# Before the experts of a two-block model: tokens transposed before their norm, a feature-major router, and a gather in full precision

## The reference, cut to what matters

```python
h = h + rms_norm(mix, post_mix_norm)
t = rms_norm(h, pre_ffn_norm)                      # x * rsqrt(mean(x*x) + eps) * gain, 256 x 1024
g_prob = softmax(t @ w_group_router + b_group)     # 4 groups
g_w, g_idx = top_k(g_prob, 1)
e_logits = (t @ w_expert_router + b_expert)        # 32 experts in 4 groups
e_w, e_idx = top_k(softmax(e_logits[group g_idx]), 2)
weights = g_w * e_w / sum(e_w)
hid = silu(t @ w_gate[e]) * (t @ w_up[e]) * weights      # experts, 1024 -> 256
routed = hid @ w_down[e]                                 # 256 -> 1024
shared = (silu(t @ w_sh_gate) * (t @ w_sh_up)) @ w_sh_down
h = h + rms_norm(routed + shared, post_ffn_norm)
```

## Time and profile before

| | |
|---|---|
| median of three runs | 1015.51 us (1015.17 to 1015.65) |
| profiled execution | 1013.33 us, its span 1011.7 us |
| busy over the span | PE 84%, DVE 52%, ACT 38%, POOL 4% |
| mean granted clock of TensorE | 0.901 of full |
| moved by DMA | 205.80 MB, mean 203 GB/s |

### The profile page before, as it was taken

How to read it: one execution, slowest core, us unless ns; L and a number is a source line. 1 busy time by engine, 2 the same in 40 slices (tenths; PEclk the granted TensorE clock), 3 DMA queues, 4 the chain that set the end, 5 groups by cost and what they waited for, 6 DMA issues and landing times.

```text
span 1011.7 us, 13380 instructions
## 1 busy us (share of the span) xinstructions
PE 848.5 (84%) x5447; PEld 665.3 (66%) x5447; DVE 525.3 (52%) x858; ACT 383.3 (38%) x635; POOL 40.2 (4%) x101
## 2 busy tenths in 40 slices
PE   5877799777867676658699999779999999999976
PEld 3877555676534343323699987548787899989964
DVE  2669841554210010201666579894577666666655
ACT  4434533433200001001645475453544543444334
POOL 3000000000111110010000000000000000000000
PEclk9889855958998987888799999798999999999988
DMA  9941102510999999999951845205555556655201
GB/s 273 386 136 42 42 1 99 187 68 1 386 417 417 415 417 417 418 418 386 286 180 43 304 155 208 94 1 197 198 163 170 167 173 204 203 170 174 77 1 42
DMA packets 82099, 205.80 MB, mean 203 GB/s; under 512 B 7836, under 2 KB 50980, under 8 KB 73844
## 3 DMA queue, kind: packets, MB, share of 16 engines
q1 hardware_dynamic: 69632, 151.46, 42.2%
q0 software_dynamic: 10064, 53.27, 13.1%
q10 hardware_dynamic: 2340, 0.18, 0.2%
HBM read 203.85 MB, written 1.05 MB: 203 GB/s over the span
## 4 chain that ended last, share of the span: by engine, by line
PE 61%; DMA 16%; DVE 15%; ACT 4%; issue 3%; POOL 0%; SPq 0%; ACTq 0%; DVEq 0%
DMA big<-in_w_gate 14%; PE ps L1797 8%; PE ps L1798 8%; PE ps L1799 8%; PE ps L1623 7%; PE ps L1625 7%; PE ps L1624 7%; PE ps L1882 4%; DMA big<-in_w_in 2%; DVE WL L1001 2%; PE ps L1741 1%; PE ps L1753 1%; DVE XT L1443 1%; DVE big L1483 1%; DVE WL L993 1%
## 5 line engine op out<-in xcount | busy, mean ns | idle before, releaser
L1001 DVE TENSOR_TENSOR WL<-big,WH 128x1024 fp32r<-128x1024 f32 x154 | 186.8, 1223 | 112.0 <-ACT WH L589 110.3
L1623 PE MATMUL ps<-XH,WH 128*128 128x256 f32 (+1 forms) x672 | 195.7, 291 | 5.4 <-DVE XL L1016 4.9
L589 ACT ACTIVATE WH<-big 128x1024 fp32r<-128x1024 f32 x154 | 160.8, 1054 | 89.5 <-PE ps L1799 88.6
L1624 PE MATMUL ps<-XL,WH 128*128 128x256 f32 (+1 forms) x672 | 193.2, 287 | 0.0
L1625 PE MATMUL ps<-XH,WL 128*128 128x256 f32 (+1 forms) x672 | 192.9, 287 | 0.0
L1623 PEld LDWEIGHTS ps<-XH,WH 128*128 128x128 f32 x672 | 130.7, 195 | 8.4 <-issue 6.1
L1624 PEld LDWEIGHTS ps<-XL,WH 128*128 128x128 f32 x672 | 130.9, 195 | 0.8
L1625 PEld LDWEIGHTS ps<-XH,WL 128*128 128x128 f32 x672 | 130.7, 195 | 0.0
L1797 PE MATMUL ps<-WH,XH 128*128 128x512 f32 x256 | 104.5, 408 | 12.0 <-DVE WL L993 5.0
L1882 PE MATMUL ps<-big 128*32 128x256 f32 x1024 | 75.3, 459 | 45.0 <-DMA big<-in_w_gate 31.1
L1798 PE MATMUL ps<-WH,XL 128*128 128x512 f32 x256 | 102.4, 400 | 0.0
(11 more groups left out here) (346 smaller groups left out, 1104.8 us busy)
## 6 DMA issues: line engine op xcount, KB each, us to landing
big<-in_w_in SPq DMA_DIRECT2D x35, 1024.0 KB, 9.2
big<-in_w_gate SPq DMA_DIRECT2D x16, 1024.0 KB, 14.8
big<-in_w_up SPq DMA_DIRECT2D x16, 1024.0 KB, 18.2
big<-in_w_gate POOLq DMA_DIRECT2D x16, 1024.0 KB, 19.3
big<-in_w_up POOLq DMA_DIRECT2D x16, 1024.0 KB, 22.7
big<-in_w_down SPq DMA_DIRECT2D x16, 1024.0 KB, 16.5
big<-in_w_down POOLq DMA_DIRECT2D x16, 1024.0 KB, 18.7
big<-in_w_mlp_up SPq DMA_DIRECT2D x16, 1024.0 KB, 5.5
```

Source lines behind the costliest of these rows:

```text
L589: s.activation(dst, src, ACT.Copy).then_inc(ev("unit_high"), 1)
L1001: v.tensor_tensor(dst, src, h.bitcast(F32), ALU.subtract).then_inc(ev("unit_split"), 1)
L1623: mm(o, h, rh, start=first, stop=False, skip_group_check=skip)
L1624: mm(o, h, rl, start=False, stop=False, skip_group_check=skip)
```

## The change

It has six parts.

1. `h_tok` plus the scaled projection is written into `h1`; the transposes read `h1` unnormed as soon as `h_mixed` counts. XH and XL hold the unnormed features times the gain. The reciprocal root `st(5)` is made once and multiplied in afterwards: into the logits, into the silu and the product of the shared expert, into the gathered rows.
2. The router is feature-major: `router_hi` and `router_lo` are the stationary side (36 columns), the 256 tokens move; 24 matmuls of 256 columns instead of 48 of 36 and the bias rows. The 36x256 result is copied to SBUF, transposed back by two small matmuls, and scaled with the bias added (`b_router` is now broadcast to 128 partitions by its two DMAs).
3. The shared units are token-major (tokens stationary, 256 hidden columns moving, again 24 matmuls a unit). `silu` and product are made by token rows, so four transposes and two copies bring the hidden rows back (`sh_turned`). `shared_unit(2)` stands behind the ranks.
4. `th` and `tl` are gone. ACT writes the normed, reordered rows into `h_tok` (L767 after), right behind the XH copies, and the gather multiplies them in float32: 16 matmuls of 256 columns for the first octet instead of 32 `fp32r` ones, and 4 instead of 8 for each of the 12 later pieces.
5. At the end of the experts the sum reads `h_tok` in the other order and times its root: `scalar_tensor_tensor` with one strided operand in place of L1395, twice; the new row stays in `ffn_tmp`, and ACT copies it to `h_tok` during units 2 and 3 of the second block.
6. The down slabs are laid `(p c)` instead of `(c p)`: one run of 8 KB for a partition instead of two of 4 KB; `turn_hidden` reads every second column to match. Many semaphores used once become counts of one per engine (`mark`).

```diff
@@ names @@
-        h1n = ar(2048, TT * D).rearrange("p (k d) -> p k d", k=TT)
+        h1 = ar(2048, TT * D).rearrange("p (k d) -> p k d", k=TT)
-        th = XH[:, 0:TT * D].rearrange("p (k d) -> p k d", k=TT)
-        tl = XL[:, 0:TT * D].rearrange("p (k d) -> p k d", k=TT)
+        by_row = lambda a: a.rearrange("p (c q) -> p q c", c=DC)
+        in_order = lambda a: a.rearrange("p (q c) -> p q c", c=DC)
-                src = A["w_down"][0][bass.ds(e, 1)].rearrange("e (c p) n -> p (e c) n", p=P)
+                src = A["w_down"][0][bass.ds(e, 1)].rearrange("e (p c) n -> p (e c) n", p=P)
@@ ACT @@
+            act.wait_ge(*mark("ffn_in_root"))
+            for t in range(TT):
+                s.activation(by_row(h_tok[:, t, :]), in_order(h1[:, t, :]), ACT.Copy, scale=st(5, t))\
+                    .then_inc(ev("t_by_row"), 1)
             u0 = FIRST1["shg"]
-            for k in range(2):
-                high1(u0 + 3 + k)
-                take1(u0 + k, sact[:, k, :], func=ACT.Silu, n=S)
+            high1(u0 + 3)
+            high1(u0 + 4)
+            act.wait_ge(ev("unit_used"), u0 + 2)
+            for t in range(TT):
+                s.activation(sact[:, t, :], ps[:, 1 + t, 0:FF], ACT.Silu, scale=st(5, t)).then_inc(ev("sh_gate"), 1)
             high1(u0 + 5)
-
-            act.wait_ge(ev("unit_used"), u0 + 4)
-            for t in range(TT):
-                s.activation(th[:, t, :].rearrange("p (c q) -> p q c", c=DC),
-                             h1n[:, t, :].rearrange("p (q c) -> p q c", c=DC), ACT.Copy).then_inc(ev("th_ready"), 1)
...
                 high2(k + 3)
+                if k in (2, 3):
+                    act.wait_ge(ev("tok_normed"), k - 1)
+                    s.activation(h_tok[:, k - 2, :], ffn_tmp[:, k - 2, :], ACT.Copy).then_inc(ev("h_kept"), 1)
@@ DVE @@
-                v.tensor_tensor(h_tok[:, t, :], h_tok[:, t, :], h1n[:, t, :], ALU.add).then_inc(ev("h_mixed"), 1)
-            for t in range(TT):
-                dve.wait_ge(ev("tok_std"), 1 * TT + t + 1)
-                chain(v.reciprocal(st(5, t), st(4, t)))
-                v.tensor_scalar(h1n[:, t, :], h_tok[:, t, :], st(5, t), None, ALU.mult).then_inc(ev("tok_normed"), 1)
+                v.tensor_tensor(h1[:, t, :], h_tok[:, t, :], h1[:, t, :], ALU.add).then_inc(ev("h_mixed"), 1)
+            dve.wait_ge(ev("tok_std"), 2 * TT)
+            v.reciprocal(st(5), st(4)).then_inc(ev("vector_mark"), 1)
...
-            dve.wait_ge(ev("logits"), 1)
+            dve.wait_ge(*mark("routed"))
             dve.wait_ge(*const("rank_or"))
-            chain(v.tensor_copy(logit, ps[:, 0, 0:2 * 36].rearrange("p (t n) -> p t n", t=TT)))
+            v.tensor_copy(logits_f, ps[0:GROUPS + EXPERTS, 0, 0:S]).then_inc(ev("vector_mark"), 1)
+            dve.wait_ge(*mark("logits"))
+            dve.wait_ge(ev("router_loaded"), 64)
+            dve.wait_ge(*mark("ffn_in_root"))
+            for t in range(TT):
+                chain(v.scalar_tensor_tensor(out=logit[:, t, :], in0=ps[:, 4, 36 * t:36 * (t + 1)], scalar=st(5, t),
+                                             in1=b_router[:], op0=ALU.mult, op1=ALU.add))
...
-            low_tok(0)
-            low_tok(1)
+            low1(u0 + 4)
+            dve.wait_ge(ev("unit_used"), u0 + 4)
+            for t in range(TT):
+                dve.wait_ge(ev("sh_gate"), t + 1)
+                v.scalar_tensor_tensor(out=sact[:, t, :], in0=ps[:, (3, 0)[t], 0:FF], scalar=st(5, t), in1=sact[:, t, :],
+                                       op0=ALU.mult, op1=ALU.mult).then_inc(ev("sh_hidden"), 1)
...
-                v.tensor_tensor(h_tok[:, t, :], h_tok[:, t, :], ffn_tmp[:, t, :], ALU.add).then_inc(ev("h_ffn"), 1)
+                v.scalar_tensor_tensor(out=in_order(ffn_tmp[:, t, :]), in0=by_row(h_tok[:, t, :]), scalar=st(4, t),
+                                       in1=in_order(ffn_tmp[:, t, :]), op0=ALU.mult, op1=ALU.add)\
+                    .then_inc(ev("h_ffn"), 1)
@@ PE @@
-                    pe.wait_ge(ev("tok_normed"), no * TT + t + 1)
+                    pe.wait_ge(ev("tok_normed" if no else "h_mixed"), t + 1)
...
             for c in range(DC):
                 pe.wait_ge(ev("turned_low"), c + 1)
-                for t in range(TT):
-                    o = ps[:, 0, 36 * t:36 * (t + 1)]
-                    tk = slice(t * P, (t + 1) * P)
-                    if c == 0:
-                        mm(o, ones[0:1, :], b_router[:], start=t == 0, stop=False, skip_group_check=True)
-                    mm(o, xh2[:, c, tk], router_hi[:, c, :], start=False, stop=False, skip_group_check=True)
-                    mm(o, xl2[:, c, tk], router_hi[:, c, :], start=False, stop=False, skip_group_check=True)
-                    last = mm(o, xh2[:, c, tk], router_lo[:, c, :], start=False, stop=c == DC - 1,
-                              skip_group_check=True)
-            last.then_inc(ev("logits"), 1)
+                last = triple(ps[0:GROUPS + EXPERTS, 0, 0:S], router_hi[:, c, :], router_lo[:, c, :], xh2[:, c, :],
+                              xl2[:, c, :], c == 0, c == DC - 1)
+            last.then_inc(ev("tensor_mark"), 1)
+            pe.wait_ge(*mark("logits_by_feature"))
+            for t in range(TT):
+                last = tr(ps[:, 4, 36 * t:36 * (t + 1)], logits_f[:, t * P:(t + 1) * P],
+                          ident[0:GROUPS + EXPERTS, 0:GROUPS + EXPERTS])
+            last.then_inc(ev("tensor_mark"), 1)
...
             shared_unit(1)
-            shared_unit(2)
-            pe.wait_ge(ev("chosen_ready"), 1)
+            pe.wait_ge(*mark("chosen_ready"))
...
-                        for part, x in enumerate((th, tl)):
-                            last = mm(o, x[:, t, c * P:(c + 1) * P], sel[:, b, t, 0:width],
-                                      start=t == 0 and part == 0, stop=t == TT - 1 and part == 1)
+                        last = mm(o, h_tok[:, t, c * P:(c + 1) * P], sel[:, b, t, 0:width].bitcast(F32),
+                                  start=t == 0, stop=t == TT - 1)
```

More of the change, by code:

```diff
@@ L735, in _ @@
                 act.wait_ge(ev("h_mixed"), t + 1)
-                s.activation(junk, h_tok[:, t, :], ACT.Square, accum_out=st(3, t)).then_inc(ev("tok_square"), 1)
+                s.activation(junk, h1[:, t, :], ACT.Square, accum_out=st(3, t)).then_inc(ev("tok_square"), 1)
                 act.wait_ge(ev("tok_square"), 1 * TT + t + 1)
@@ L1857, in _ @@
             mm(o(2), ones[:], r_m[:, 0, :], start=True, stop=False)
-            mm(o(2), ones[:], r_m[:, 1, :], start=False, stop=True).then_inc(ev("ranks"), 1)
+            mm(o(2), ones[:], r_m[:, 1, :], start=False, stop=True).then_inc(ev("tensor_mark"), 1)
+            shared_unit(2)
             shared_unit(3)
```

129 lines of the change are left out of this document (70 added, 59 removed).

## The result

The changed kernel takes 1001.24 us (median; 999.92 to 1005.37 in four runs), the kernel before beside it 1015.34 (1013.85 to 1015.65): a ratio of 0.987 with an interval of 0.9851 to 0.9889. The profiled execution took 1000.23 us, its span is 998.5 with a mean clock of 0.911. A second series of the changed kernel, further down, gave 1001.36.

A forecast was written before the change was run, and what follows sets the result against it. In the experts slab transfers set the pace, so savings before the first gate product count one to one. 14.4 - 1.7 + 1.2 - 0.7 = 13.2 us off 1013.33, plus 2.2 for the median, gave 1002.3; range 999.5 to 1009.

The forecast's parts named there:

- What bounds the kernel: In the experts slab transfers set the pace; time lost or saved before the first gate product counts one to one.
- The chain up to the gate product: Steps from the last row added to the first gate product, which was to start 14.4 us earlier.
- high parts: ACT's high parts ahead of the router, to begin at 208.97 instead of 211.00, 2.0 us earlier.
- choice: DVE's choice from the router's logits, to be made at 221.15, where it was made at 229.34 before.
- The float32 product priced by the combination's records: First gather: 0.45 us per float32 product of 256 columns, 7.2 us for 16, against 5.9 measured before.
- The clock's fall: TensorE's drop to half speed, expected at 209.9 behind the second transposes, with full speed again from 213.9.
- the rival: The clock never falls ahead of the router, which ends 1.5 us earlier; 1000.8 us, chance 0.12.
- Pieces of later gathers: Dearer float32 pieces, 0.85 us each, show only for two in the first quad: 1.7 us back (0 to 2.6).
- Down slabs: Expert down weights in runs of 8 KB might quicken the transfers: 1.2 us gained, bounds 0 to 3.
- The stride: Sum behind the experts reads one operand at a stride, twice: 0.7 us lost, upper bound 1.3.
- G to C: Stretch from first gate product to last combination of the experts, 0.5 us longer by the terms for pieces and slabs.
- The sum: Total saving of all terms in the kernel: 14.4 - 1.7 + 1.2 - 0.7 = 13.2 us.

The follow-up runs named there:

- e5: Changed kernel with the first gather's 16 float32 products made twice; 1008.5 us.
- e6: Changed kernel with each float32 piece of a later gather issued twice from the second quad on; 997.97 us (one run).
- e2: Changed kernel with the router's tokens stationary and 36 columns moving again, 48 products, without the copy and transposes back; 1009.4 us (one run).
- e3: Changed kernel whose transposes again wait for each row's root and scaling, the scaled product written aside; 1006.21 us (one run).
- e11: Changed kernel with the gather alone back to two reduced parts, made from the reordered rows behind the last shared unit; 1004.03 us.
- e12: Changed kernel with the five rank products behind the third shared unit again; 1001.24 us (one run).
- e10: Changed kernel with pauses filled by useless products, high parts ahead of the second root, first row added in order, and 22 more filler products; 997.86 us.
- e1: Changed kernel with the down slabs laid as before, in runs of 4 KB, and hidden columns read in order; 1004.51 us.
- e7: Changed kernel where ScalarE copies the first row back into token order, so its sum is a plain addition; 999.96 us (one run).
- e9: Changed kernel with 36 useless products filling TensorE's pauses between the mixer's end and the router; 1004.1 us (five runs).
- e8: Changed kernel with e7's edit, high parts ahead of the second row's root and VectorE's reciprocal behind the low parts; 1000.83 us (one run).

## Why the prediction was right

**What bounds the kernel.** Right: the first gather twice moved everything behind it by its own 6.9 us, and doubled pieces in the running stream moved nothing (e5, e6).

**The chain up to the gate product.** Right step by step, behind M: second transposes predicted at 5.5, measured 5.6; high parts 7.0 and 6.9; clock down at 7.9 and up at 11.9, measured 5.2 (in the pause) and 12.0; router's end 12.6 and 12.8; choice 19.2 and 19.5; last unit 26.2 and 26.5; gather's end 33.4 and 33.6; gate product 34.4 and 34.6. The float32 product priced by the combination's records (7.2 us) took 7.07. The clock's fall is the one step that went another way: it came 5.2 us behind M, where the kernel before had it too (207.05 - 201.98 = 5.1), and I had it fall behind the second set, so that this set would run at full speed; it ran at half. It cost 0.9 us more there, of which ScalarE's root hid nearly all. Without the clock's fall the stretch would be 1.6 us shorter, which the rival had at 1.5. On this the Trainium skill (TensorE: Matmul & The Clock Gate, HAM oscillation) says that idle gaps of more than a certain length bring the clock down. The trace agrees that pauses do it, since filling them keeps it up; but here a pause of 3.04 us, 1.06 us of work and a second pause were enough.

**Where the 14.3 us are.** 6.2 in the form of the router (e2), 1.3 in the norm behind the transposes (e3), 2.3 in the unsplit gather (e11), nothing in the place of the ranks (e12). The other 4.5 no edit takes apart, but the traces account for nearly all of them. In 2.2 of them the high and low rows of before held up the gather for 5.77 us at strides, where the same from rows already in order took 3.61. The narrow router of before took 11.66 us from its first matmul to its last, that of e2 10.40: 1.3 us for the bias rows that are gone. And its first matmul came 10.16 us behind M, in e2 8.00. Nothing of these 2.2 us is hidden, since the clock came back in neither kernel while the router ran: 0.9 us more than the norm cost in e3.

**Pieces of later gathers.** Right in size: in the first 40 us behind the gate product the changed kernel moved 18 GB/s less than the kernel before, 0.73 MB, 1.7 us of the stream (1.4 in the second series); the sum had 1.7. But dearer pieces alone are not the cause, and neither is the clock alone. In e10, e6 and e2, with the same float32 pieces and the clock up, the stretch moves 380, 374 and 380 GB/s; with split pieces and the clock down for 3.4 us it moves 374 (before) and 380 (e11); with float32 pieces and the clock down 351 to 365, in all nine profiles of that kind. It is the pieces and the half clock together, which the sum, with its price at full speed, did not have.

**Down slabs.** The mechanism that I had left open is the one that acts, and the term was mis-sized: 1.2 us in the sum, 2.0 by the rate (e1), 2.6 to 2.9 in that experiment's profile, inside its bounds of 0 to 3.

**The stride.** This term was mis-sized: 0.7 us in the sum, 2 x 0.74 = 1.5 by the rows, above the upper bound of 1.3 as well, where the bound came from an operation with one input less (L1209). Of it 0.94 us reached the second block's transposes; 0.4 us were taken up by VectorE's wait for the first root, 1.21 us in place of 1.59. The Trainium skill (SBUF — State Buffer, Door 1: The DMA port swizzle) says that float32 elements further apart than one 16-byte line pay. The trace agrees that the stride costs (1.97 against 1.22 us in e7), and the bound of 1.3 us would have been nearer than 0.7.

**G to C.** 0.5 us longer in the sum, 0.8 and 1.1 measured. The volume moved 190 us behind G is level (77.5 MB before, 77.4 and 77.6 after), so pieces and slabs cancel by then; what remains shows in the last quad, where the up product starts 9.95 us behind the gate product instead of 8.29. Why the last up slabs land later while the down slabs are quicker, no run tells.

**The sum.** 14.3 - 0.8 - 0.9 = 12.6 us by the stretches that the change touches, 13.2 predicted. The profiles differ by 13.1 (and by 12.3 with the second series): the rest is M and the tail, which vary by themselves. In the first profile M came 2.5 us later than before and the tail was 3.0 shorter; that these nearly cancel is luck, and so is a part of the nearness of the median, forecast at 1002.3, at 1001.2 and 1001.4.

## What to carry to other kernels

Write a small projection so that the long operand streams: 24 products of 256 columns in place of 48 of 36 did more than any other single edit here (6.2 us): they are half as many, and the clock came back during them. A transposition of rows doesn't need their norm: what scales a whole row can be applied behind every product. And measure by distances from an event ahead of the change; the five totals of e9, one and the same kernel, lie 8 us apart.

## What the runs showed of the hardware

TensorE busy without a break for ten microseconds with products of 36 columns stayed at 1.2 GHz (e2), and the same work in products of 256 columns came back to 2.4 GHz 4.0 us (changed), 1.2 us (e12) or 1.0 us (e8) into it. Two pauses of 3.04 and 1.50 us with 1.06 us of work between them brought it down to 1.2 GHz, in e11 and e12 it fell in the first of them already, 2.3 and 2.4 us behind M instead of 5.2. A pause of 3.1 us between the first gate product and the first later piece was followed by a fall in the changed kernel (at 247.2) and by none in e6 and e2, so the pause's length alone doesn't decide. Products without a use that filled such pauses kept it at 2.4 GHz.

A float32 product of 256 columns takes 7.07 / 16 = 0.44 us at 2.4 GHz, 3.7 times the 0.12 us of a reduced one. An operation of VectorE on 1024 float32 elements takes 1.22 to 1.28 us in order and 1.97 with one input and the output at a stride of 8 elements. Weights fetched in runs of 8 KB instead of 4 KB, a third of the traffic, raised the rate of all from 417 to 421 GB/s.
